# Routing and the seam to the experts in an encoder layer with hierarchical mixture of experts: order of the gates, of the first index column, of the gather and of the first split

## The reference

```python
h = h + mixer(rmsnorm(h, p['ln_mix_g']), cos, sin, p)
h = h + hier_moe(rmsnorm(h, p['ln_ffn_g']), p)
...
grp = jnp.argmax(grp_logits, axis=-1)                      # 4 groups of 8 experts
p_grp = take_along_axis(softmax(grp_logits), grp)
in_grp = exp_logits of the 8 experts of that group
top_v, top_i = lax.top_k(in_grp, 2)
gates = softmax(top_v) * p_grp
eid = grp * 8 + top_i
...
hid = silu(xb @ w_g[e]) * (xb @ w_u[e])                    # xb: the rows of expert e
y[token] += gate * (hid @ w_d[e])
```

## Time and profile before

| what | us |
|---|---|
| median of the timed runs (3) | 1344.29 (1342.59 to 1349.86) |
| profiled execution | 1334.59 |
| its span | 1332.9 |
| TensorE busy in it | 1201.6 (90%) |
| VectorE busy | 891.6 (67%) |
| ScalarE busy | 852.5 (64%) |
| GpSimd busy | 284.8 (21%) |

### The profile page before, as it was taken

The page is one execution under the profiler, slowest core; times in us unless marked ns, Lnnn a source line. Parts: engine busy times, 40 slices in busy tenths (PEclk is TensorE's granted clock), DMA queues, the critical chain, the costliest instruction groups (busy, mean ns, idle before and its releaser), DMA issues.

```text
span 1332.9 us, 21871 instructions
## 1 busy us (share of the span) xinstructions
PE 1201.6 (90%) x5939; PEld 1010.1 (76%) x5939; DVE 891.6 (67%) x1112; ACT 852.5 (64%) x1017; POOL 284.8 (21%) x264
## 2 busy tenths in 40 slices
PE   4999999964999999994599999999999999999972
PEld 3998888963787888883488888888888888787851
DVE  5574456343566666756478886565788888888874
ACT  6438888453556666554468775465677778777772
POOL 1000000013122222211103322223332233323320
PEclk9999999965999999996699999999999999999996
DMA  5251110076133322343499988797999999999985
GB/s 188 96 213 40 39 39 16 0 265 165 57 94 87 96 83 83 116 177 118 182 349 392 378 326 307 246 329 261 348 389 381 379 382 387 379 376 366 397 303 231
DMA packets 68854, 302.06 MB, mean 227 GB/s; under 512 B 12027, under 2 KB 22780, under 8 KB 44242
## 3 DMA queue, kind: packets, MB, share of 16 engines
q1 hardware_dynamic: 50994, 262.97, 51.1%
q0 software_dynamic: 17824, 38.66, 11.7%
HBM read 264.57 MB, written 44.43 MB: 232 GB/s over the span
## 4 chain that ended last, share of the span: by engine, by line
PE 41%; DMA 19%; issue 6%; DVE 4%; POOL 3%; ACT 2%; POOLq 2%; DVEq 0%; ACTq 0%; SPq 0%
DMA h_dram<-y_sb,ix_y 15%; PE ps L1967 13%; PE ps L2004 8%; PE ps L1233 7%; PE ps L1190 4%; PE ps L1163 2%; DMA ex<-u_dram,ix_x 2%; POOL ix_x L1876 2%; PE ps L1174 2%; PE ps L1958 1%; POOLq L1807 1%; PE ps L1213 1%; PE ps L1185 1%; POOL ex L1887 1%; PE ps L1990 1%
## 5 line engine op out<-in xcount | busy, mean ns | idle before, releaser
L2134 DVE TENSOR_TENSOR d_lo<-raw_w_down,d_hi 128x2048 fp32r<-128x2048 f32 x62 | 139.3, 2288 | 49.8 <-ACT d_hi L2038 49.8
L2134 DVE TENSOR_TENSOR g_lo<-raw_w_gate,g_hi 128x2048 fp32r<-128x2048 f32 x64 | 143.8, 2288 | 33.4 <-ACT g_hi L2038 33.2
L2134 DVE TENSOR_TENSOR u_lo<-raw_w_up,u_hi 128x2048 fp32r<-128x2048 f32 x64 | 143.9, 2288 | 13.0 <-ACT u_hi L2038 13.0
L2038 ACT ACTIVATE g_hi<-raw_w_gate 128x2048 fp32r<-128x2048 f32 x64 | 119.1, 1909 | 8.3 <-issue 8.3
L595 PE MATMUL pj<-h_hi,w_hi 128*128 128x432 f32 x336 | 123.3, 367 | 0.1
L595 PE MATMUL pj<-h_lo,w_hi 128*128 128x432 f32 x336 | 120.7, 359 | 0.0
L595 PE MATMUL pj<-h_hi,w_lo 128*128 128x432 f32 x336 | 120.3, 358 | 0.0
L2038 ACT ACTIVATE u_hi<-raw_w_up 128x2048 fp32r<-128x2048 f32 x64 | 118.9, 1906 | 1.1 <-DMA raw_w_up<-in_w_up 1.1
L1967 PE MATMUL ps<-g_hi,ex_hi 128*128 128x512 f32 x280 | 113.1, 404 | 5.3 <-DVE ex_lo L2150 5.3
L2038 ACT ACTIVATE d_hi<-raw_w_down 128x2048 fp32r<-128x2048 f32 x62 | 115.1, 1907 | 0.1
L1967 PE MATMUL ps<-u_hi,ex_hi 128*128 128x512 f32 x280 | 113.5, 405 | 0.0
(11 more groups left out here) (295 smaller groups left out, 2702.7 us busy)
## 6 DMA issues: line engine op xcount, KB each, us to landing
raw_w_gate<-in_w_gate SPq DMA_DIRECT2D x64, 1024.0 KB, 9.4
raw_w_up<-in_w_up SPq DMA_DIRECT2D x64, 1024.0 KB, 9.1
raw_w_down<-in_w_down SPq DMA_DIRECT2D x64, 1024.0 KB, 10.9
k_win<-k_dram POOLq DMA_DIRECT2D x20, 384.0 KB, 5.7
w_raw<-in_w_in SPq DMA_DIRECT2D x14, 512.0 KB, 4.1
late_dram<-a_g SPq DMA_DIRECT2D x11, 512.0 KB, 6.5
xh<-in_x SPq DMA_DIRECT2D x10, 512.0 KB, 3.4
h_dram<-xh SPq DMA_DIRECT2D x10, 512.0 KB, 2.7
```

What stands on the lines that cost most here:

```text
L2038: act.activation(hi[c][:, :], raw[c][:, :], ACT.Copy).then_inc(hi_done, 1)
L2134: dve.tensor_tensor(lo[c][:, :], raw[c][:, :], hi[c][:, :].bitcast(F32), ALU.subtract).then_inc(lo_done, 1)
```

## The change

It moves instructions and splits two of them; nothing is computed that was not computed before, except that the index column of block 0 is read by a transfer of its own.

1. ScalarE: the copies of heads 0 to 3 come before the two exponentials of the routing, those of heads 4 to 7 behind.
2. VectorE: the four gate operations leave `route` and stand behind both residuals, ahead of `place`.
3. TensorE, drain: the router product of block 8 stands behind the first six attention products; the turns of block 9 stand inside the drain, one behind the ranking and one at the end; `route` waits for the two halves of u_t apart.
4. VectorE, last step: `ffn_scale` of block 9 comes behind `place`.
5. VectorE, seam: the split of the first gate weights comes before the plan; the split of x comes before that of the ups.
6. SP: `ix_x` of block 0 is read from `list_dram` by its own small transfer; then the lists, then the table; the weights of block 1 also wait until x has arrived; g_final is read behind the weights of block 1.
7. GpSimd: the first gather waits for that small transfer alone, without a copy.
8. x of block 0 is split by halves, and the first gate product waits for its halves apart.

```diff
@@ TensorE, step of mix
-            if b2 is not None:
+            last = t is None and b1 is None
+            drain = t is None and b1 is not None
+            if b2 is not None and not last:
                 turn_u(b2, 0, s)
...
-            if b2 is not None:
+            if b2 is not None and not drain:
                 route(b2)
             for i in range(2):
                 for j in range(2):
                     if b1 is not None:
                         out_product(b1, 1, i, range(2 * j, 2 * j + 2))
-                    if t is None and b2 is not None and b1 is not None and (i, j) == (1, 0):
+                    if drain and (i, j) == (0, 0):
+                        route(b2)
+                    if drain and (i, j) == (1, 0):
                         place(b2)
+                        turn_u(b1, 0, 1 - s)
+                    if drain and (i, j) == (1, 1):
+                        turn_u(b1, 1, 1 - s)
@@ ScalarE, step of mix
                 sink_and_rec(t)
+                probs_out(t, range(0, 4))
             if b2 is not None:
                 route(b2)
             if t is not None:
-                probs_out(t, range(HEADS))
+                probs_out(t, range(4, HEADS))
@@ VectorE, step of mix
-                route(b2, s)
+                route(b2)
             if b1 is not None:
                 residual(b1, 1 - s, 1, 0)
                 residual(b1, 1 - s, 1, 1)
             if b2 is not None:
+                gates_of(b2, s)
                 place(b2, s)
+            if t is None and b1 is None:
+                ffn_scale(b2, s)
@@ experts, SP
-        sp.dma_start(lists[:, :, :], list_dram.rearrange("(p c) o -> p c o", p=P)).then_inc(lists_in, 16)
-        sp.dma_start(g_final[:, :], a["ln_final_g"][0].partition_broadcast(P)).then_inc(g_in, 16)
+        by_slot = list_dram.rearrange("(p c) o -> p c o", p=P)
+        sp.dma_start(ix_x[:, :], by_slot[:, 0, :]).then_inc(first_listed, 16)
+        sp.dma_start(lists[:, :, :], by_slot).then_inc(lists_in, 16)
+        store_table(sp)
         sp.wait_ge(table_in, 16)
+        sp.wait_ge(x_in, 16)
+        sp.sem_inc(waited_sp, 1)
         load_new(1, a["w_gate"], KG, gates)
...
         load_new(1, a["w_down"], KDN, downs)
+        sp.dma_start(g_final[:, :], a["ln_final_g"][0].partition_broadcast(P)).then_inc(g_in, 16)
@@ experts, GpSimd
+        gather(0)
         pool.wait_ge(lists_in, 16)
-        gather(0)
@@ experts, VectorE
         split(0, gates)
+        make_table(dve)
+        dve.wait_ge(x0_hi_done, 1)
+        dve.tensor_tensor(x_lo[:, 0:KG, :], ps_x[:, 0, :]..., x_hi[:, 0:KG, :].bitcast(F32),
+                          ALU.subtract).then_inc(x0_lo_done, 1)
+        dve.wait_ge(x_hi_done, 1)
+        dve.tensor_tensor(x_lo[:, KG:KD, :], ps_x[:, 1, :]..., x_hi[:, KG:KD, :].bitcast(F32),
+                          ALU.subtract).then_inc(x_lo_done, 1)
         split(0, ups)
-        x_split(0)
         split(0, downs)
```

57 lines of the change are left out of this document (38 added, 19 removed).

## The result

The changed kernel is faster, by about 1.5%. Its four runs have a median of 1319.7 us (1318.0 to 1332.3), beside 1344.7 us of four runs of the kernel before. Over all runs the ratio of the two kernels is put at 0.9855 with a 95% interval of 0.9806 to 0.9904 (the medians alone make 0.981), which on 1344.29 us makes 1324.8 us. One of those six executions took 2047.5 us at a mean granted clock of 0.56; it stands in their median and not in the ratio. The forecast was 1330.4 us, with 1322 to 1338 as its range. The profiled execution took 1318.01 us, of which 1316.3 are its span; the forecast for it was 1320.7.

The account below looks back on a forecast made before the run. TensorE was taken as the bound from about 660 us, with holes in the attention loop and the seam before. Loop -2.8, drain 0 and seam -11.1 made -13.9 us: 1344.29 to 1330.4 us, range 1322 to 1338.

Parts of the forecast that it names:

- Part 1: Attention loop: with four copies ahead of ScalarE's routing exponentials, four long steps lose their excess, -4.9 us.
- Part 2: Attention loop: VectorE's gates behind the last residual lose 0.30 us in each of seven steps, +2.1 us.
- Part 3: Drain: TensorE's new order gains nothing, 0 us, with -1.1 and +0.8 as ends.
- Part 4: Last block on VectorE: gates run beside the ranking, k_pre waits till afterwards, addr ends 0.87 us earlier.
- Part 5: Seam: GpSimd's scatters are slowed by VectorE's work, a cost; GpSimd gets in between two splits, second scatter ends at 626.4.
- (e): Seam: the scatters lose to both splits, +2.3 us, 1332.7 us; counted within the forecast's 0.65.
- Part 6: Seam: index column takes 2.1 us, gather issues 0.85 us later and lands in 4.1 us instead of 9.4; x in at 634.7.
- (a): Seam: the gather's 9.4 us are its own, going first doesn't shorten it; -8.6 us, 1335.7 us, chance 0.12.
- Part 7: Seam: x by halves takes 2.4 us to the first gate product, which starts 11.1 us earlier.
- (b): Attention loop: VectorE is the bound, gates cost their whole 0.78 us in seven steps; -10.5 us, 1333.8 us, chance 0.07.
- (c): Last router product and first gate products run at the higher clock; 4.0 us more gained, 1326.4 us, chance 0.09.
- (d): Expert stage: limited by the stream of weights, which starts 4.9 us later; +3.4 us, 1347.7 us, chance 0.05.

Follow-up runs that it names:

- m2_one_wait: Changed kernel with the router product waiting once for both halves of the copied block; second to last product with v took 224.62 us, 1.97 longer.
- m3_gates_early: Changed kernel with VectorE's gates ahead of the residuals again in steps with a block t; second to last product with v took 221.10 us, 1.55 shorter.
- m1_copies_last: Changed kernel with all eight probability copies behind the two routing exponentials again; second to last product with v took 227.08 us, 4.4 longer.
- d1_drain_old: Changed kernel with TensorE's old drain order; last product with v to start of last router product took 23.73 us, 1.57 shorter.
- s4_scale_first: Changed kernel with u scaled ahead of the last block's gates and place; end of hot to first gate product took 20.09 us, 1.71 more.
- s5_gather_beside: Changed kernel with the first gather held until block 1's gate weights were asked for; the gather landed in 5.9 us, against 4.3.
- after_again: The changed kernel timed once more, unedited: 1322.9 us, ratio 0.9858 to the kernel before.
- s3_x_whole: Changed kernel with x of block 0 split whole; end of hot to first gate product took 20.33 us, 1.95 longer.
- b1_all: Changed kernel with gates early, old TensorE drain, plan before gate split, and that split's second half behind the gather: 1316.3 us, ratio 0.9805 to the kernel before.

## Why the prediction was right or wrong

**Bound.** Right in the main: what the first expert gained arrived at the end (684.5 and 684.3 us). Not quite right that TensorE is the bound throughout; see the last section.

**Part 1**, -4.9. Undone it costs 4.4. Mechanism as read: the exponential's wait for ediff. That the 4.4 lie so near the 4.9 is partly luck: they are two held steps and six short losses, not four held steps. The rows held no hint of the 0.25 us in the steps that weren't held, and the forecast didn't ask why ediff was long.

**Part 2**, +2.1. Undone it gives 1.55 back; 0.30 us a step was right, but five steps lost it and a sixth 0.11, not seven.

**The term that was missing.** "Parts 1 and 2 make -2.8": the loop gained 5.8. The missing term is the third edit of the diff, the router product's wait for its halves apart. It stood under part 3 as a matter of the drain, and its worth in the loop was never asked, though TensorE's weight load had 0.25 to 0.32 us of idle time ahead in each step: 1.97 us by m2_one_wait. With it the three experiments make -4.43 + 1.55 - 1.97 = -4.9; the last 0.9 us of the 5.8 belong to none of the edits alone. They lie between part 1 and the split wait: m3_gates_early differs from the kernel before in column 1 by these two only and is 7.34 us shorter there, where the two undone singly make 6.40. With one wait `ediff` meets `rec_lo` in four steps, with the split wait in two, so m1_copies_last, which has the split wait, shows part 1 at less than it is worth in the kernel before. That this makes up the whole 0.9 us fits and is not shown. The forecast of 28.3 us a step was 27.9 in the trace.

**Part 3**, 0 in the forecast, +0.4 in the traces. Right as a number, by luck. At the full clock the order costs 1.57 us and the gates 0.79, together 2.4. The trace of before had a dip of the clock in just this stretch, worth 2.5 us in column 2, which I had not looked up, so its times were no measure of the old order. "The last residual 0.6 to 0.9 us earlier" came true for the same reason only: it starts 22.95 us behind the last product with v in the trace of before and 22.08 in the changed kernel, but 20.50 in d1_drain_old. Against the old order at the full clock it is 1.6 us later, because TensorE's wait for `hot` sits ahead of the products that feed it.

**Part 4**, -0.87. `addr` came 0.80 us earlier than with the old order. Right; its worth turned out double (1.71 us in s4_scale_first), by which operation the scatter then meets.

**Part 5**, second scatter 2 us long and between two splits. 1.88 us. It started at 619.00 and ended at 620.88, 0.87 behind the middle of the pair, the first one 0.85 behind k_pre's end. The long issues shown here, those of the earlier trace rows included, end 0.83 to 0.97 us behind an operation of VectorE on whole tiles. The order of two waiting instructions stays what the row at 702.31 of the earlier trace rows showed: GpSimd gets in between. (e) falls. The Trainium skill (SBUF — State Buffer, section "SBUF: two separate sides") has the ports that VectorE and GpSimd share as an exclusive lock: an operation of VectorE with two SBUF inputs, or one of GpSimd that reads SBUF, holds it for the whole instruction, whichever starts first. The long issues agree with that, and so does `ediff` beside `rec_lo`. One thing in the trace is milder than a full lock: where a second half of the split follows, as behind the scatter at 619.00, the last 0.87 us of the issue run beside it, and the pair of halves still takes 4.48 us.

**Part 6.** Right. Column 1.6 us (2.1 forecast), gather 4.3 (4.1), and 1.1 us between column and issue (0.85). The weights were asked for 19.5 us behind `hot`, where the forecast has 18.4, since the table's write took 3.5 us beside the gather instead of 1.7 (1.8 in s5_gather_beside, where the gather hadn't begun); TensorE waited for none of them. Rival (a) falls by s5_gather_beside. No run takes the column alone back, so the 4.3 us by which the gather is issued earlier are read from the two traces and not from an experiment. Of the 5.3 us that the forecast gave to the empty engines, 1.1 were the gather's shorter issue.

**Part 7.** Right: 2.73 us from the turn to the gate product, 2.4 forecast (0.98 and 1.3 make 2.3, so 0.1 of that is a slip); whole 4.55.

**Rivals.** (b) falls: 0.30 us a step, not 0.78. (c) came in small: the first gate product took 7.93 us instead of 8.37, and the router product was slower, not faster. (d) falls.

**From the profile to the median.** The forecast was carried over to the median with the gap of the kernel before, 9.7 us between profiled execution and median, as if it were the same for both kernels. In the changed kernel the gap is 1.7 us. So of the 10.7 us between the forecast and the raw median 2.7 lie in the profiled executions and 8.0 in this gap. The gap is drawn by chance: single executions differ by more than that with the same code. By the ratio the kernel is 5.6 us below the forecast. One slip in the chances: (d) at 0.05 and the remainder of 0.03 make 0.08 within, not 0.07.

## What to carry to other kernels

Ask of every edit in a diff what it does in each place that runs it: a wait split in two for the drain was worth 2 us in the loop. Before a stretch of the old trace is taken as the price of the old order, look up the granted clock there. And where GpSimd issues an indirect transfer on the critical path, choose what VectorE runs beside it: small operations, or at least the end of a large one; moving the large one away from one issue may put it on the next. A tiny operation that is long in some steps only is worth a look at what the other engine runs beside it at that moment.

## What the runs showed that I had not expected

**The clock differs between executions at one place.** Up to the first product with v all profiles agree within 3 us. Then the second attention step takes 27.0 us in eight of them and 32.8 to 34.2 in the other six, with the same code. Windows of 332 to 346 us, the changed kernel and after_again:

```profile
332.00:346.00 14.00, 13.47 (x86) 12.02 (x85) 8.23 (x20) 6.55 (x13) 1.49 (x1) 1.00 0.00 0
```

```profile
332.00:346.00 14.00, 14.00 (x62) 13.49 (x61) 4.53 (x10) 2.30 (x4) 1.49 (x1) 0.56 0.00 0
```

Ahead of it, between projection and attention, TensorE is busy for only 12 of the 30 us from 300 on, and the clock falls to 0.50, which is 1.2 GHz; it is back by 332 us in one case and near 345 us in the other. What decides is open. The profiled executions of before and of the changed kernel both took 27.0 us there, so their difference holds none of this.

**The expert stage isn't bound by TensorE alone.** Column 5 spreads from 681.4 to 690.0 us. Most blocks take 18.1 us in every profile; a few near the start and near the end take 19 to 23, at places that partly change from run to run. TensorE's waits from 650 to 1240 us in the changed kernel and in s3_x_whole:

```profile
PE ps L1983 <- DMA ex<-u_dram,ix_x: 4.1, 4, 2.0
```

```profile
PE ps L1983 <- DMA ex<-u_dram,ix_x: 7.4, 3, 3.0
...
PE ps L1996 <- DVE ex_lo L2178: 2.8, 1, 2.8
```

Now and then a gather beside the weights lands too late (3.2 to 11.0 us in b1_all), and in s3_x_whole the wait of 3.0 us that ended at 745 us was followed by four microseconds at a clock of 0.61 and 0.54 (windows of 746 to 748 and 748 to 750 us). The window of 900 to 1000 us, on which the forecast rested, happened to hold none; a wider stretch would have shown it in the trace of before too (4.2 us in 3 waits). The clock ahead of the loop (5.8 to 7.2 us) and column 5 (8.6 us between its ends) are together as large as the spread of 14 us between the timed executions, though how they fell in each of those is not known. That is a reason not to judge edits of 1 or 2 us by the time of one run.
